# Experts' outputs: weighted and added onto x in memory by the scatter itself, in place of scatter, load and weighted sum

## The reference, cut to what matters

```python
def moe_ffn(h, router_w, router_b, w_in, w_out):
    ...
    top_p, top_e = lax.top_k(in_group, TOP_K)
    top_w = top_p / jnp.sum(top_p, axis=-1, keepdims=True)
    ...
    for e in range(N_EXPERTS):
        gu = t @ w_in[e]
        act = jax.nn.silu(gu[:, :D_EXPERT]) * gu[:, D_EXPERT:]
        y = y + gates[:, e:e + 1] * (act @ w_out[e])
```

## Time and profile before

| | us |
|---|---|
| median of 3 runs | 1619.91 |
| lowest, highest | 1617.14, 1620.81 |
| the profiled execution, its own time | 1616.9 |
| its span, first to last instruction | 1614.8 |
| busy: PE, DVE, ACT, POOL | 1451.3, 977.9, 770.5, 142.8 |
| granted TensorE clock, mean, as a share of full speed | 0.951 |
| moved by DMA | 274.96 MB, mean 170 GB/s |

### The profile page before, as it was taken

How to read it: one execution, slowest core, us unless ns; L and a number is a source line. 1 busy time by engine, 2 the same in 40 slices (tenths; PEclk the granted TensorE clock), 3 DMA queues, 4 the chain that set the end, 5 groups by cost and what they waited for, 6 DMA issues and landing times. The chain is left out here.

```text
span 1614.8 us, 19652 instructions
## 1 busy us (share of the span) xinstructions
PE 1451.3 (90%) x7753; PEld 1221.7 (76%) x7753; DVE 977.9 (61%) x1297; ACT 770.5 (48%) x1124; POOL 142.8 (9%) x159
## 2 busy tenths in 40 slices
PE   6999698879899888799999599999999896999993
PEld 5788566667688666799997478887887585999982
DVE  4473657574646436699996522455244526999974
ACT  3412555374424424577774233432143524877761
POOL 1000011200000000222211000000000002222210
PEclk9999799879999999899999799999999997999997
DMA  6723121032252043799986532321522064899965
GB/s 195 138 57 107 36 72 53 1 105 95 74 213 79 27 151 144 258 381 374 376 340 238 189 105 81 102 79 53 186 67 77 1 243 185 338 368 387 373 257 207
DMA packets 111005, 274.96 MB, mean 170 GB/s; under 512 B 41777, under 2 KB 44226, under 8 KB 106306
## 3 DMA queue, kind: packets, MB, share of 16 engines
q1 hardware_dynamic: 95506, 203.96, 36.5%
q10 hardware_dynamic: 5904, 52.96, 8.3%
q0 software_dynamic: 9504, 16.80, 2.8%
HBM read 266.27 MB, written 25.17 MB: 180 GB/s over the span
## 5 line engine op out<-in xcount | busy, mean ns | idle before, releaser
L185 DVE TENSOR_TENSOR w_lo<-w_stage,w_hi 128x2048 fp32r<-128x2048 f32 (+2 forms) x32 | 67.2, 2104 | 187.3 <-ACT w_hi L175 177.4
L175 ACT ACTIVATE w_hi<-w_stage 128x2048 fp32r<-128x2048 f32 (+2 forms) x36 | 63.9, 1780 | 235.0 <-PE bank L240 154.9
L200 DVE TENSOR_TENSOR w_lo<-w_stage,w_hi 128x2048 fp32r<-128x2048 f32 x42 | 96.1, 2289 | 62.0 <-ACT w_hi L194 36.1
L194 ACT ACTIVATE w_hi<-w_stage 128x2048 fp32r<-128x2048 f32 x38 | 72.7, 1915 | 101.6 <-PE bank L240 65.3
L2871 PE MATMUL bank<-e_wi_lo,e_hx_hi 128*128 128x384 f32 x256 | 86.7, 339 | 0.0
L2870 PE MATMUL bank<-e_wi_lo,e_hx_hi 128*128 128x384 f32 x256 | 86.6, 338 | 0.0
L240 PE MATMUL bank<-w_hi,h_sg_hi 128*128 128x512 f32 x192 | 76.6, 399 | 4.1 <-DVE h_sg_lo L2293 2.1
L2726 DVE TENSOR_TENSOR e_wi_lo<-e_room,w_hi 128x1536 fp32r<-128x1536 f32 x40 | 68.6, 1752 | 11.6 <-ACT w_hi L2722 11.4
L240 PE MATMUL bank<-w_hi,h_sg_lo 128*128 128x512 f32 x192 | 75.3, 392 | 0.0
L240 PE MATMUL bank<-w_lo,h_sg_hi 128*128 128x512 f32 x192 | 75.3, 392 | 0.0
L2730 POOL DMA_INDIRECT e_tok<-moe_h,moe_slots x32 | 64.7, 2021 | 114.3 <-DVE moe_slots L2430 78.5
(11 more groups left out here) (529 smaller groups left out, 4194.2 us busy)
## 6 DMA issues: line engine op xcount, KB each, us to landing
e_room<-in_moe_w_in SPq DMA_DIRECT2D x88, 768.0 KB, 10.5
w_stage<-in_moe_w_in SPq DMA_DIRECT2D x40, 768.0 KB, 8.3
e_wo<-in_moe_w_out ACTq DMA_DIRECT2D x16, 1536.0 KB, 10.7
e_room<-in_moe_w_out ACTq DMA_DIRECT2D x14, 1536.0 KB, 11.1
w_stage<-in_x_wkv SPq DMA_DIRECT2D x16, 1024.0 KB, 5.3
w_stage<-in_sg_w_in SPq DMA_DIRECT2D x16, 1024.0 KB, 5.2
w_stage<-in_hyb_w_in SPq DMA_DIRECT2D x10, 1024.0 KB, 5.1
w_stage<-in_x_wq SPq DMA_DIRECT2D x8, 1024.0 KB, 5.1
```

Source lines behind the costliest of these rows:

```text
L175: act.activation(self.w_hi[h][:, :, :cols], self.stage[h][:, :, :cols], ACT.Copy)\
L185: dve.tensor_tensor(self.w_lo[h][:, :, :cols], self.stage[h][:, :, :cols], self.w_hi[h][:, :, :cols], ALU.subtract).then_inc(self.lo_done[ ...
L194: act.activation(self.w_hi[h][:, :, :cols], self.stage[h][:, :, :cols], ACT.Copy).then_inc(self.hi_done[h], 1)
L200: engine.tensor_tensor(self.w_lo[h][:, :, :cols], self.stage[h][:, :, :cols], self.w_hi[h][:, :, :cols], ALU.subtract).then_inc(self.lo_do ...
```

## The change

`Combine` goes, with `moe_y`, the eight loads and the 16 weighted additions; `Summed` takes its place. x is stored to memory before the experts run (layer 0: a new tensor; layer 1: the output itself), four stores in the front. The routing weights are stored too (`w_dram`, 1024 x 1), and POOL gathers the weight of each row of each block into a column of `sw`. The evictions multiply by that column. The scatter goes to rows of x with an adding transfer, and each one waits for the landing of the one before, since a token's two experts may be in neighbouring blocks. After the last scatter layer 0 loads four tiles of x; after layer 1 nothing is left to do.

```diff
@@ Summed, in place of Combine
+    def put_x(self, engine, res, t):
+        res.wait(engine, t)
+        engine.dma_start(self.acc[t * P:(t + 1) * P, :], self.m.x[:, t, :]).then_inc(self.m.x_put, 16)
+
+    def load(self, engine, tiles):
+        for t in tiles:
+            engine.dma_start(self.m.x[:, t, :], self.acc[t * P:(t + 1) * P, :]).then_inc(self.m.x_in[t], 16)
...
@@ sgu_layer
-                    combine.landed(sp)
...
-                    combine.add(dve, 0, 0)
-                    combine.add(dve, 0, 1)
-                    combine.add(dve, 1, 0)
+                    nt.normalize(dve, 0)
                     for i in range(T):
-                        nt.normalize(dve, i)
                         if i + 1 < T:
-                            combine.add(dve, i + 1, 1)
-                        if i + 2 < T:
-                            combine.add(dve, i + 2, 0)
+                            nt.normalize(dve, i + 1)
                         rest(i)
@@ moe_front, SP
+                summed.put_x(sp, res, 0)
+                summed.put_x(sp, res, 1)
                 for t in range(T):
+                    if t + 2 < T:
+                        summed.put_x(sp, res, t + 2)
                     sp.wait_ge(nt.normed, t + 1)
                     sp.dma_start(h_dram[t * P:(t + 1) * P, :], xn[:, t, :]).then_inc(stored, 16)
@@ moe_experts
+        def weights_landed(engine, b):
+            engine.wait_ge(m.sw_in[b % 2], 16 * (MAXB // 2 * layer + b // 2 + 1))
@@ SP
+                    sp.dma_start(summed.w_dram.rearrange("(j p) o -> p (j o)", p=P), m.wgt[:, :]).then_inc(m.w_put, 16)
...
+                    sp.wait_ge(stored[1], 16 * (NE // 2))
+                    summed.load(sp, (0, 2))
@@ POOL
                 def scatter(b, buf, index):
-                    pool.indirect_dma_start(out=y_dram, ...
+                    pool.indirect_dma_start(out=summed.acc, out_offset=bass.IndirectOffsetOnAxis(ap=index, axis=0),
+                                            in_=y[:, buf, :], in_offset=None, bounds_check=S - 1,
+                                            oob_is_err=False, compute_op=ALU.add).then_inc(stored[buf], 16)
+                def weights(b):
+                    pool.indirect_dma_start(out=sw[:, b:b + 1], out_offset=None, in_=summed.w_dram,
+                                            in_offset=bass.IndirectOffsetOnAxis(ap=slots[:, 1, b:b + 1], axis=0),
+                                            bounds_check=2 * S - 1, oob_is_err=False).then_inc(m.sw_in[b % 2], 16)
...
+                pool.memset(sw[:, :], 0.0).then_inc(sw_set, 1)
+                pool.wait_ge(sw_set, 1)
+                pool.wait_ge(m.w_put, 16 * (layer + 1))
+                for b in range(4):
+                    if b >= 2:
+                        weights_landed(pool, b - 2)
+                    weights(b)
+                pool.wait_ge(m.x_put, 16 * T * (layer + 1))
                 for b in range(L - 1):
                     if b + 4 < NE:
                         pool.wait_ge(h_turned, 2 * (b + 3))
                         w.gather(pool, b + 4, b % 2, slots[:, 0, b + 4:b + 5], h_dram)
+                        weights_landed(pool, b + 2)
+                        weights(b + 4)
+                    if b == L - 3:
+                        pool.wait_ge(listed, 2)
+                        for e in range(2):
+                            weights_landed(pool, NE - 2 + e)
+                        for e in range(NE, MAXB):
+                            weights(e)
                     pool.wait_ge(y_act, b + 1)
                     pool.wait_ge(y_dve, b + 1)
-                    scatter(b, b % 2, slots[:, 1, b:b + 1])
+                    if b:
+                        pool.wait_ge(stored[(b - 1) % 2], 16 * ((b - 1) // 2 + 1))
+                    scatter(b, b % 2, slots[:, 0, b:b + 1])
+                for e in range(2):
+                    weights_landed(pool, MAXB - 2 + e)
+                pool.wait_ge(stored[1], 16 * (NE // 2 - 1))
                 with pool.Fori(0, rest(pool)) as i:
+                    pool.tensor_copy(wx[:, 0:1], sw[:, bass.ds(i + L - 1, 1)]).then_inc(wx_set, 1)
...
@@ ACT, and DVE in the same way
-                    act.activation(y[:, j, 0:GC], y_ps[0][:, :], ACT.Copy).then_inc(y_act, 1)
+                    act.activation(y[:, j, 0:GC], y_ps[0][:, :], ACT.Copy, scale=weight).then_inc(y_act, 1)
...
                 def finish_of(b):
                     act.wait_ge(wo_used, b + 1)
+                    weights_landed(act, b)
...
                     act.wait_ge(stored[0], i * 16 + 16 * (NE // 2 - 1))
-                    finish(0)
+                    act.wait_ge(wx_set, i + 1)
+                    finish(0, wx[:, 0:1])
                     act.wait_ge(wo_los, L - 1)
                     act.dma_start(wo[1][:, :, :], ...
@@ build_trunk
-        store_x(m, combine, out)
+                acc = nc.dram_tensor("moe0_x", [S, D], F32).ap()
+            combine = moe(m, layer, at[f"xo{layer}"], o, o_ctx, right[layer], None if layer else at["sgu"], out[0] if layer else acc)
```

More of the change, by code:

```diff
@@ L276, in _ @@
             pool.wait_ge(made, 6)
[L280 to L297, removed]
 def nsa_outputs(m, c):
@@ L1632, in add, with __init__ @@
         dve.tensor_tensor(m.x[:, t, GC:D], m.x[:, t, GC:D], m.psum[4 + t][:, :], ALU.add).then_inc(self.added, 1)
[L1635 to L1646, removed]
+class Summed:
+    def __init__(self, m, layer, gain_row, acc, w_dram):
+        self.m, self.gain_row, self.acc, self.w_dram, self.layer = m, gain_row, acc, w_dram, layer
+    def put_x(self, engine, res, t):
[4 more added lines that the diff above has]
+            engine.dma_start(self.m.x[:, t, :], self.acc[t * P:(t + 1) * P, :]).then_inc(self.m.x_in[t], 16)
     def load_gain(self, engine, gain):
         engine.dma_start(self.gain_row, gain.partition_broadcast(P)).then_inc(self.m.next_gain_in, 16)
[L1651 to L1659, removed]
-    def wait(self, engine, t):
[L1662 to L1670, removed]
+    def wait(self, engine, t):
+        engine.wait_ge(self.m.x_in[t], 16)
 class Arrival:
@@ L2786, in _ @@
             def _(sp):
+                with nc.allow_non_contiguous_dma(reason="one weight per token"):
+                    sp.dma_start(summed.w_dram.rearrange("(j p) o -> p (j o)", p=P), m.wgt[:, :]).then_inc(m.w_put, 16)
                 sp.wait_ge(w.hx_in[1], 16)
@@ L2803, in _ @@
                     sp.wait_ge(wo_used, L)
-                    combine.load_gain(sp, m.a["norm_mix"][layer + 1])
-                sp.wait_ge(stored[1], 16 * (NE // 2))
-                combine.load(sp, 0)
+                    summed.load_gain(sp, m.a["norm_mix"][layer + 1])
+                    sp.wait_ge(stored[1], 16 * (NE // 2))
+                    summed.load(sp, (0, 2))
             @block.gpsimd
@@ L3040, in _ @@
                 act.wait_ge(stored[1], 16 * (NE // 2 - 1))
-                finish(1)
-                act.wait_ge(stored[1], 16 * (NE // 2))
-                combine.load(act, 1)
+                act.wait_ge(wx_set, n + 1)
+                finish(1, wx[:, 1:2])
+                if upcoming is not None:
+                    act.wait_ge(stored[1], 16 * (NE // 2))
+                    summed.load(act, (1, 3))
             @block.vector
@@ L3157, in _, with moe @@
                 dve.wait_ge(stored[1], 16 * (NE // 2 - 1))
[L3158 to L3161 removed]
+                dve.wait_ge(wx_set, n + 1)
+                finish(1, wx[:, 1:2])
+def moe(m, layer, first, o, o_ctx, kv_ctx, upcoming, acc):
     nm = f"moe{layer}"
     h_dram = m.nc.dram_tensor(f"{nm}_h", [S, D], F32).ap()
[L3165 removed]
+    w_dram = m.nc.dram_tensor(f"{nm}_w", [2 * S, 1], F32).ap()
     with ExitStack() as c:
@@ L3169, in moe @@
         rt = Routing(m, c, layer)
-        combine = Combine(m, layer, w.rows, w.gain_row, y_dram)
+        summed = Summed(m, layer, w.gain_row, acc, w_dram)
         o_ctx.close()
-        moe_front(m, layer, w, slots, m.wgt, rt, h_dram, first, o)
+        moe_front(m, layer, w, slots, m.wgt, rt, h_dram, first, o, summed)
         kv_ctx.close()
-        moe_experts(m, layer, w, slots, rt, h_dram, y_dram, combine, upcoming)
-    return combine
+        moe_experts(m, layer, w, slots, rt, h_dram, summed, upcoming)
+    return summed
 def build_trunk(nc, a, out):
```

36 lines of the change are left out of this document (17 added, 19 removed).

## The result

The changed kernel took 1657.04 us (median of 4 runs, 1655.35 to 1661.87) against 1619.64 us for the kernel before beside it: a ratio of 1.0241, 95% interval 1.0228 to 1.0254. It is 37 us slower; the forecast was 1616.5, with a range that ended at 1643. The profiled execution took 1657.34 us, with a span of 1655.3 (before: 1616.9 and 1614.8).

The account below looks back on a forecast made before the run. TensorE was taken to bound the expert stage with DMA close behind, and memory traffic the tail. Terms -17.3 - 1.4 + 14.3 + 1 = -3.4 us against the median of 1619.91 gave 1616.5 us, range 1601.5 to 1643.

Parts of the forecast that it names:

- expert stages: Adding scatters read their rows too, on the loaded half of the DMA engines; late loads stop PE 7.2 us per layer: +14.3.
- entrance of the loop: Ahead of the loop over empty blocks, eight overflow weights gathers and a new wait for scatter 13: 0.5 us a layer, +1.
- turn: Layer 0 to layer 1: two additions ahead of the first square go, the adding scatter gives 1.3 us back: net -1.4 us.
- end: After layer 1's last scatter, 18.9 us of loads, additions and store go; adding scatter 1.3, block end 0.3: net -17.3 us.
- Storing the 4 KB of weights is one SP issue of about 1 us: SP's store of the routing weights, ahead of a load that waits for a gather anyway: costs nothing.
- The rule cited from the Trainium skill: An add in the DMA path needs two source reads and halves the rate: about 0.16 us more a row, sum within 1 us.
- 872 + 1.5 + 2.4 + 3.5 = 879.4: Entrance of the loop: scatter 13's landing, then the empty block's gather, against PE's turn at 878.54: 0.5 us a layer.
- wrong altogether: Sign that the forecast fails: PE stalls at the stage's start or empty block by over 3 us, or the front gets longer.
- from the second tile on PE is the bound there: Turn of the layers: only the time up to the first norm's square changes, within the net -1.4 us.
- 0.3 us for the end of the block: Cost put on the end of the block after layer 1's last adding scatter, within the net -17.3 us.
- Hidden, nothing: Costs put at nothing: x's stores in the front, weights gathers within the stage, scaled evictions, waits for the scatter before.
- the dear addition: Rival: 0.34 us more a row makes weights late, stage term 40 us, without a chain of scatters: 1642 us, chance 0.13.

Follow-up runs that it names:

- experiment 2: Changed kernel with plain scatters in place of adding ones, all waits, weights gathers and orders kept: 1624.13 us (ratio 1.0041 to the kernel before).
- experiment 3: Changed kernel with one iota pattern altered so a block's rows are borne by 16 DMA engines in place of 8: 1637.05 us (ratio 1.0120).
- experiment 10: Change in layer 1 alone, rows over 16 engines, scatter wait moved, overflow gathers split; weights now stored as 128 rows of 32 bytes: 1603.25 us (ratio 0.9908).
- experiment 4: Changed kernel with the wait for block 13's scatter moved to the loop's own scatter and the 8 overflow weights gathers split in two: 1649.79 us.
- experiment 5: experiment 3 without the gathers of weights and the waits for them, routing weights set to 0.5 throughout: 1621.65 us (ratio 1.0025).
- experiment 1: Changed kernel with DVE's order in layer 1's sgu put back, normalize(i) and then rest(i): 1647.97 us (ratio 1.0183).
- experiment 7: Kernel before the change with the altered iota, its blocks' rows borne by 16 DMA engines in place of 8: 1614.47 us (ratio 0.9979).
- experiment 11: Change in both layers with DVE's order put back, rows over 16 engines, moved wait with split gathers, weights stored as 128 rows: 1605.82 us (ratio 0.9930).
- experiment 8: Changed kernel with the repairs of experiment 1, experiment 3 and experiment 4, plus the weights' store issued on ACT's queue: 1622.82 us (ratio 1.0032).

## Why the prediction was wrong

| term | forecast | measured in the span |
|---|---|---|
| up to layer 0's first silu | 0 | +1.7 |
| expert stages, two layers | +14.3 | +20.1 |
| entrance of the loop, two layers | +1 | +14.3 |
| turn, with all of the way to layer 1's first silu | -1.4 | +15.1 |
| end | -17.3 | -10.7 |
| sum | -3.4 | +40.5 |

The forecast had the sign wrong: not faster by 3.4 us but slower by 40.5. Two steps failed in their mechanism, the entrance and the turn; the stage and the end were mis-sized.

- **The expert stage**: mechanism and price right. An addition was priced at 0.17 us, from a gathered row; experiment 2 gives 0.17 to 0.18. That half of the engines bear all of it was read off and is shown by experiment 3. Silu 1 to 14 got 9.8 and 7.1 us longer, against 7.2 a layer. What was missing is the start, from silu 0 to 1: "Storing the 4 KB of weights is one SP issue of about 1 us" counted the issue and not the 1024 elements. In the changed kernel the start is 0.7 us longer in layer 0 and 2.5 in layer 1; experiment 10 takes the whole of it away in layer 1. The rule cited from the Trainium skill ("Collectives: The Full Stack", Part 3), two source reads for an add, fits the stage, where an adding row comes to some 0.34 engine-us against 0.17, twice. It does not give what a scatter by itself shows: 0.45 engine-us a row (22.7% of 16 engines over 7.5 us, 61 rows) against 0.17 for the plain one of experiment 2, or 2.6 times. (By the rule's ratio the forecast would have been an estimated 2 us lower, not within 1 us of it.)
- **The entrance**: the step that failed is "872 + 1.5 + 2.4 + 3.5 = 879.4", worth 0.5 us. It took each time from the trace of before. But the gathers start only when the late stage lets them, the first and the scatter behind them took 3.7 and 3.9 us, and scatter 13 landed after 9 us and not 6. I also named `wx_set` and did not follow it: the copy stands behind the new wait, and so an eviction and a `w_out` load do. PE's stall at the empty block was 6.4 us, twice the 3 us that the prediction named as a sign of being wrong altogether. Experiments 4 and 5 part the two: the place of the gathers in layer 0, the wait in layer 1. With plain scatters the same gathers and the same wait cost 1.8 and 0.3 us (experiment 2): it takes the order of POOL's program and the longer landing together.
- **The turn**: "from the second tile on PE is the bound there" failed. It left out a line of the diff, the order of `normalize` and `rest`, that removes nothing and adds nothing. PE then waits 10.3 us for `h_sg_lo`. It cost 12.6 of the 15.1 us at the place, 9.1 of the median (experiment 1). Up to the first square the turn got 1.9 us longer, not 1.4 shorter: the two additions saved their 2.7, but the loads behind the scatter went out 6.1 us after its issue, not 3.2 (892.60 in the earlier trace rows), and the DRAIN, 2.0 longer, stands ahead of ACT's table load.
- **The end**: too large by 6.6 us. "0.3 us for the end of the block" was 4.56 us of DRAIN, of which 2.60 stood in the trace of before, hidden beside the loads, and 1.96 come with the gathers of weights (experiment 5); the landing cost 1.9 us more than priced (6.6 to the DRAIN, with 3.4 before and 1.3 forecast on top).
- **Hidden, nothing**: right for the front (from POOL's last routing operation to the first gather it is 39.9 us in place of 39.8 in layer 0 and 39.8 in place of 39.5 in layer 1; the rest of layer 0's first 1.7 us stands ahead of the stores of x), right for the gathers within the stage's blocks, and nearly right for the scaled evictions, each of which got longer (0.68 us in place of 0.60 on ACT, 0.75 in place of 0.69 on DVE). The wait for the scatter before decided at scatter 13 alone; in the stage's blocks the chain stayed apart, with landings of 9.9 us.

Of the rivals the dear addition (1642 us) was nearest, by its sum only; its mechanism was not what happened. Missed were two losses that the price of a transfer alone could not have given: an order in DVE's program, and what stands behind a late landing in POOL's.

Left open: why a lone adding row takes 0.45 engine-us and one in the stage about 0.34; why the first gap of a stage differs so between kernels (10.9 to 15.4 us with the same store); how the DRAIN grows with the number of indirect transfers, of which the runs have two values only; and the 1 to 3 us by which layer 0's first silu moves between kernels that differ only behind it.

## What to carry to other kernels

In these runs an adding scatter paid at the end of the last layer, where nothing follows it (experiment 10 is 11 us under experiment 7); in layer 0, with all repairs, it gained nothing (experiment 11). Before blaming the sum of DMA work, ask which engines bear it: rows that fill half of the partitions load half of the engines, and one iota pattern was worth 20 us here. And in a diff read the moved lines as closely as the new ones: for each wait and each transfer, say what stands behind it on its engine.

## What the runs showed of the hardware that I had not expected

- A DRAIN at the end of a Block takes 2.60 us on POOL, and 4.56 us in a layer with 24 more gathers, 0.08 us for each in the mean, whether the scatters are plain or adding (experiments 2 and 5).
- An adding scatter mostly takes POOL 1.6 us to issue, a plain one 1.0 us.
- A store of 4 KB in 1024 elements landed after 15 to 22 us, beside other work, and SP took 7.00 us, not 1.65, to issue the three loads behind it; in 128 rows it landed after 1.4 us. The Trainium skill ("DMA: Bandwidth & Descriptors", Rules for kernel authors) has it that a last dimension that isn't contiguous becomes one descriptor per element; the runs agree, with 874 more packets under 512 B for 1024 elements in place of 128 rows (1398 against 524 in experiment 10). It also says (Issuing engines are not separate DMA queues) that transfers issued by different engines run on the same 16 DMA engines and interleave there; experiment 8 agrees, since the store moved to ACT's ring was no better out of the way and cost 11.8 us.
